# Scores of the grouped heads from split queries and keys, and the convolution's taps moved among the heads

## The chip, the cores and the metric

One core of a Trainium2 chip runs the whole program. The metric is the device time of one execution in microseconds (us). Engines: TensorE (PE, with its weight loads as PEld), VectorE (DVE), ScalarE (ACT), GpSimd (POOL), SyncE (SP). Each takes its own instructions strictly in order; they meet at semaphores.

## The reference

The program is two blocks in a row, for 256 tokens of width 1024. The change is in the second block's layers. There a token stream is projected into four branches; two of them are attention, one is a depthwise convolution:

```
qg, kg, vg = ...                       # 8 query heads, 2 key/value heads, 64 wide ("grouped")
qm, km, vm = ...                       # 8 heads, queries and keys 96 wide ("latent")
o = softmax(q @ concat(k_ctx, k).T * scale) @ concat(v_ctx, v)      # both kinds
conv[t] = b + sum over tap of w[tap] * glu[t + tap - 15]            # 31 taps, 512 channels
x = x + g1 * merge(conv, gate, o_m, o_g);   x = x + g2 * conv_ffn(x)
```

Over two layers three such stages run in full: the context stream of layer 0 (256 keys, no rotary embedding), the main stream of layer 0 and the main stream of layer 1 (both 512 keys, rotary). A fourth, shorter stage has no attention.

## The kernel before

Everything is feature-major: features on the 128 partitions, tokens along the free axis. Weights come by DMA into a ring of three tiles; ACT makes a high part of each half tile (L1839) and DVE the low part (L2583), both in the type fp32r, and TensorE forms high*high + high*low + low*high, three fp32r matmuls in place of one of fp32 (`three`, L825). The trace has two records for each fp32 matmul and one for each fp32r matmul.

`stream(t)` is written three times, once for each engine, and works through one stage; its order is written by hand. `n` counts the full stages, `HEADS` is 16, `MH` is 8: heads j = 0 to 7 are latent, 8 to 15 grouped. `taps(...)` below is `depthwise_conv`. The loop over heads, by engine:

- TensorE: `scores(j)` (L1545) multiplies the queries of two token halves (a stationary of 96 or 64 rows) with the keys (256 or 512 columns), in fp32, into two of six PSUM banks that three heads share in turn; `turn(j)` (L1562) transposes the exponentials; `weigh` (L1579) multiplies with the values, four matmuls of 256 columns at 512 keys and two at 256 keys. Iteration j does turn(j), scores(j+2), weigh for earlier heads. `scores(j+2)` waits until ACT has copied out head j-1. After head 7 and after head 15, `shares` (L1555) transposes the inverse sums: it waits for DVE's `inverse_sums`. scores(10) takes the banks of the first `shares`, and waits until ACT has copied these (`spread_shares`, L2284).
- DVE: `row_max(j+2)` (L3178, L3179), then at set places the splitting of weights (L2583), `inverse_sums` (L3192, L3193), `weighed_heads` (L3199), `low_part` (L3184), and then taps of the depthwise convolution (L3089), one `scalar_tensor_tensor` of 128x256 for each tap and block of 128 channels; each tap of a block adds to the one before.
- ACT: for head j, the copy of the turned head to SBUF (L2303), then the two exponentials of head j+2 (L2291).

Before: `row_max(j+2)` stands ahead of iteration j's taps, `inverse_sums(0)` in iteration 7 ahead of `row_max(9)`, and `inverse_sums(1)` behind the loop. In the rotary stages the taps end with iteration 12: one tap of blocks 0 to 2 in each of iterations 0 to 7, one of block 3 in most of these, four of block 3 in each of iterations 8 to 12. In the stage without rotary only block 3 is left for the loop: two taps in most iterations, three in 10 to 12.

Of the kernel before, what the change touches and what calls it, by code (L numbers as in the profile page):

```python
# [7 lines left out]
F32R = mybir.dt.float32r  # L8
# [6 lines left out]
P = 128  # L15
# [187 lines left out]
def build(nc, d, out, ffn_tiles, stream_tiles):  # L203
# [3 lines left out]
    with ctx:  # L207
# [43 lines left out]
        latent_parts = [parts("latent_high", 25088, 4, S), parts("latent_low", 26112, 4, S)]  # L251
        grouped_parts = [parts("grouped_high", 27264, 4, S), parts("grouped_low", 28288, 4, S)]
        conv_parts = [parts("conv_high", 20992, 4, S), parts("conv_low", 22016, 4, S)]
        branch_parts = [parts("branch_high", 27264, KT, S), parts("branch_low", STREAM_H_AT, KT, S)]
# [331 lines left out]
        def _(pe):  # L586
# [833 lines left out]
            def stream(t):  # L1420
# [117 lines left out]
                def scores(j):  # L1538
                    q, k, _, _ = head(j)
                    if j >= 3:  # L1540
                        pe.wait_ge(s["at_pt"], base + j - 2)
                    if j == MH + 2:
                        pe.wait_ge(s["at_norm"], 5 * n + 2)
                    for tt in range(NT):
                        mm = pe.matmul(ps[:, two_banks(j) + tt, 0:keys], q[:, tt * P:(tt + 1) * P], k, start=True, stop=True)  # L1545
                    mm.then_inc(s["at_s"], 1)
# [19 lines left out]
                def weigh(j, part):  # L1566

                    pe.wait_ge(s["at_pt"], base + j + 2)
                    if j == MH // 2 and 0 in part:
                        pe.wait_ge(s["mm_evac"], mm_n[0])  # L1570
                    if j == MH and 0 in part:

                        pe.wait_ge(s["part_high"], 8 * n + 1)
                    for c in part:
                        for i in (j, j + 1):
                            _, _, b, half = head(i)
                            o = ps[half * HD:(half + 1) * HD, 6 + b // 2, (b % 2) * S:(b % 2 + 1) * S]
                            v = v_m[:, c, i * HD:(i + 1) * HD] if i < MH else v_g[:, c, half * HD:(half + 1) * HD]
                            mm = pe.matmul(o, v, pT[i % 4][:, c, :], start=(c == 0), stop=(c == keys // P - 1), skip_group_check=True)  # L1579
                            if c == keys // P - 1:  # L1580
                                mm.then_inc(s["at_o"], 1)
# [52 lines left out]
                def branch(number, moving, behind=None):  # L1634
                    pe.wait_ge(s["part_low"], 7 * n + number)
                    for p in range(4):
# [25 lines left out]
                upper = [split_block() for _ in range(KT)]  # L1662
                pe.wait_ge(s["part_low"], 7 * n + 5)
                for k in range(4):
# [4 lines left out]
                for q in (2, 3):  # L1669
                    pe.wait_ge(s["part_low"], 7 * n + 4 + q)  # L1670
                    for k in (2 * q, 2 * q + 1):
                        mm = out_product(0, 0, k, upper[k], False)
                    if q == 3:

                        mm.then_inc(s["half_used"], 1)
                    for k in (2 * q, 2 * q + 1):
                        mm = out_product(0, 1, k, lower[k], False)
# [26 lines left out]
        def _(actv):  # L1704
# [466 lines left out]
            def stream(t):  # L2171
# [127 lines left out]
                for j in range(HEADS):  # L2299
# [5 lines left out]
                    if j == MH + 3:  # L2305
                        actv.wait_ge(s["part_high"], 8 * n + 1)
                        a(latent_parts[0][:], weighed, ACT.Copy).then_inc(s["part_high"], 1)
                    if j + 2 < HEADS:
                        exponentials(j + 2)
                    if j == 1:  # L2310
                        keep_last_gates()
                actv.wait_ge(s["part_low"], 7 * n + 1)
                spread_shares(1, two_banks(HEADS))
# [47 lines left out]
        def _(dve):  # L2361
# [693 lines left out]
            def stream(t, mm):  # L3055
# [125 lines left out]
                def low_part(number, into, whole, ms=slice(0, 4)):  # L3181

                    dve.wait_ge(s["part_high"], 8 * n + 1 + number)
                    stt(out=into[1][:, ms, :], in0=whole[:, ms, :], scalar=1.0, in1=into[0][:, ms, :], op0=ALU.mult, op1=ALU.subtract)\  # L3184
# [10 lines left out]
                def weighed_heads(group):  # L3195
# [3 lines left out]
                    tt(weighed, attended, weighed, ALU.mult).then_inc(s[("part_high", "at_norm")[group]], 1)  # L3199

                depthwise_conv((3,), range(4))
                row_max(0)
                lows(t, 45)
                row_max(1)
                for j in range(HEADS):
# [8 lines left out]
                    if j == HEADS - 3:  # L3214
                        low_part(1, latent_parts, weighed)
                    if t["rope"] and j < MH:
                        depthwise_conv((0, 1, 2), range(23 + j, 24 + j))
                        if j != 3:
                            depthwise_conv((3,), range(4 + j - (j > 3), 5 + j - (j > 3)))
                    elif t["rope"] and j < HEADS - 3:  # L3220
                        depthwise_conv((3,), range(11 + 4 * (j - MH), 15 + 4 * (j - MH)))
                    elif not t["rope"] and j != 3 and j < HEADS - 3:
                        depthwise_conv((3,), range(4 + 2 * (j - (j > 3)) + max(0, j - 10), 6 + 2 * (j - (j > 3)) + max(0, j - 9)))
                inverse_sums(1)
# [199 lines left out]
```

## Time and profile before

| | |
|---|---|
| time, 3 runs | median 2585.94 us, 2576.88 to 2588.35 |
| the profiled execution | 2578.61 us, span 2576.8 us, granted clock 1.00 |
| busy: PE, PEld, DVE, ACT, POOL | 2541.6, 2361.9, 2050.4, 1282.6, 58.3 us |
| chain that ended last | PE 86%, DVE 9%, ACT 4%, issue 1%, DMA 0% |
| head loops (first scores to second shares) | about 1270 to 1313, 1728 to 1795, 2246 to 2312 us |

The stages of layer 0 (context), layer 0 (main) and layer 1 (main) are called stage 0, 1 and 3 below. A timeline row gives start, busy time, engine, line and tile, and how many instructions it merges. Instructions of one engine overlap at their ends, so what one costs its engine in a full queue is the distance from its start to the next start. That distance is called its step.

### The profile page before, as it was taken

The numbers are of one execution on the slowest core, as the hardware profiler recorded it, in microseconds if no ns is written. First come the engines' busy times: TensorE is split into PE (matmuls) and PEld (weight loads), VectorE is DVE, ScalarE is ACT, GpSimd is POOL, SyncE is SP. The second block draws the span as 40 slices with busy tenths as digits, with TensorE's granted clock in tenths as the row PEclk, the third lists the DMA queues.
The fourth block names the chain that finished last, engine by engine and source line by source line (L and its number), as shares of the span: only waits on it lengthen the run. The fifth ranks groups of instructions, "written<-read, shape, count | busy, mean of one in ns | idle before, by whom it ended". The sixth has DMA issues, their size and how long they took to land.

```text
span 2576.8 us, 49677 instructions
## 1 busy us (share of the span) xinstructions
PE 2541.6 (99%) x20050; PEld 2361.9 (92%) x20050; DVE 2050.4 (80%) x3059; ACT 1282.6 (50%) x1767; POOL 58.3 (2%) x72
## 2 busy tenths in 40 slices
PE   8999999999999999999999999999999999999999
PEld 8999799999988889998979999885999988859999
DVE  7996589899876369967887876797887877978877
ACT  5445553353353344355565445546544465465543
POOL 0000000000011000000000000000000000000000
PEclk9999999999999999999999999999999999999999
DMA  7764267677532067753424555340355543404554
GB/s 294 287 233 173 90 241 281 236 266 276 217 113 101 18 255 260 262 191 137 164 82 166 193 181 194 131 164 9 140 196 188 187 150 146 164 1 148 196 180 146
DMA packets 61518, 454.60 MB, mean 176 GB/s; under 512 B 6872, under 2 KB 6896, under 8 KB 9280
## 3 DMA queue, kind: packets, MB, share of 16 engines
q1 hardware_dynamic: 54720, 394.24, 42.6%
q0 software_dynamic: 6656, 58.35, 5.8%
q8 instruction: 104, 1.70, 0.3%
q14 instruction: 38, 0.31, 0.0%
HBM read 451.49 MB, written 1.07 MB: 176 GB/s over the span
## 4 chain that ended last, share of the span: by engine, by line
PE 86%; DVE 9%; ACT 4%; issue 1%; DMA 0%; DVEq 0%; SPq 0%; ACTq 0%
PE ps L825 20%; PE ps L658 15%; PE ps L659 15%; PE ps L660 15%; PE ps L1119 3%; PE ps L1545 2%; DVE w_parts L2378 1%; PE ps L1404 1%; DVE half_parts L2583 1%; PE ps L1562 1%; PE ps L600 1%; PE ps L1579 1%; PE ps L1387 1%; PE ps L1472 1%; PE ps L1416 1%
## 5 line engine op out<-in xcount | busy, mean ns | idle before, releaser
L1752 ACT ACTIVATE w_parts<-ring 128x1024 fp32r<-128x1024 f32 x462 | 463.1, 1052 | 370.3 <-PE ps L658 347.8
L658 PE MATMUL ps<-normed_parts,w_parts 128*128 128x256 f32 x2160 | 603.3, 279 | 1.7 <-DVE w_parts L2378 1.7
L659 PE MATMUL ps<-normed_parts,w_parts 128*128 128x256 f32 x2160 | 603.5, 279 | 0.0
L660 PE MATMUL ps<-normed_parts,w_parts 128*128 128x256 f32 x2160 | 602.7, 279 | 0.0
L2378 DVE SCALAR_TENSOR_TENSOR w_parts<-ring,w_parts 128x1024 fp32r<-128x1024 f32 x462 | 544.7, 1220 | 30.8 <-ACT w_parts L1752 30.3
L825 PE MATMUL ps<-stream_high,half_parts 128*128 128x256 f32 x2288 | 437.5, 287 | 3.2 <-DVE half_parts L2583 2.2
L658 PEld LDWEIGHTS ps<-normed_parts,w_parts 128*128 128x128 f32 x2160 | 405.9, 188 | 2.3 <-DVE w_parts L2378 2.3
L660 PEld LDWEIGHTS ps<-normed_parts,w_parts 128*128 128x128 f32 x2160 | 406.0, 188 | 0.0
L659 PEld LDWEIGHTS ps<-normed_parts,w_parts 128*128 128x128 f32 x2160 | 405.9, 188 | 0.0
L825 PEld LDWEIGHTS ps<-stream_high,half_parts 128*128 128x128 f32 x2288 | 358.5, 188 | 9.5 <-issue 7.9
L2583 DVE SCALAR_TENSOR_TENSOR half_parts<-ring,half_parts 128x1024 fp32r<-128x1024 f32 x225 | 272.1, 1214 | 116.1 <-ACT half_parts L1839 115.5
L658 PE MATMUL ps<-act_parts,w_parts 128*128 128x256 f32 x1232 | 344.6, 280 | 0.8 <-DVE w_parts L2378 0.8
L659 PE MATMUL ps<-act_parts,w_parts 128*128 128x256 f32 x1232 | 344.2, 279 | 0.0
L660 PE MATMUL ps<-act_parts,w_parts 128*128 128x256 f32 x1232 | 343.7, 279 | 0.0
L1839 ACT ACTIVATE half_parts<-ring 128x1024 fp32r<-128x1024 f32 x225 | 235.4, 1058 | 187.8 <-PE ps L825 160.7
L825 PE MATMUL ps<-stream_low,half_parts 128*128 128x256 f32 x1144 | 319.5, 279 | 0.0
L2465 DVE CUSTOM_DVE_ANT_0 arena<-arena 128x1024 f32<-128x1024 f32 x192 | 227.2, 1221 | 7.7 <-DVE vec L2545 6.5
L658 PEld LDWEIGHTS ps<-act_parts,w_parts 128*128 128x128 f32 x1232 | 231.5, 188 | 2.0 <-issue 1.5
L660 PEld LDWEIGHTS ps<-act_parts,w_parts 128*128 128x128 f32 x1232 | 231.6, 188 | 0.0
L659 PEld LDWEIGHTS ps<-act_parts,w_parts 128*128 128x128 f32 x1232 | 231.5, 188 | 0.0
L825 PEld LDWEIGHTS ps<-stream_low,half_parts 128*128 128x128 f32 x1144 | 215.4, 188 | 4.3 <-issue 4.1
L3089 DVE SCALAR_TENSOR_TENSOR arena<-arena,vec 128x256 f32<-128x256 f32 x360 | 154.2, 483 | 2.4
(495 smaller groups left out, 3807.1 us busy)
## 6 DMA issues: line engine op xcount, KB each, us to landing
ring<-in_weights SPq DMA_DIRECT2D x373, 1024.0 KB, 4.8
arena<-in_mod_weights POOLq DMA_DIRECT2D x32, 1536.0 KB, 6.9
arena<-in_cond POOLq DMA_DIRECT2D x8, 512.0 KB, 7.5
arena<-toeplitz_rows POOLq DMA_DIRECT2D x1, 1536.0 KB, 10.5
x<-in_x SPq DMA_DIRECT2D x1, 1024.0 KB, 4.9
arena<-in_ctx POOLq DMA_DIRECT2D x1, 1024.0 KB, 5.5
out<-x SPq DMA_DIRECT2D x4, 256.0 KB, 2.6
arena<-in_rope POOLq DMA_DIRECT2D x1, 640.0 KB, 8.7
```

The source lines that it names most:

```text
L658: first = pe.matmul(into, wh, high, start=start, stop=False, skip_group_check=True)
L659: pe.matmul(into, wh, low, start=False, stop=False, skip_group_check=True)
L660: return first, pe.matmul(into, wl, high, start=False, stop=stop, skip_group_check=True)
L825: mm = pe.matmul(into, stationary, moving, start=start and n == 0, stop=stop and n == 2, skip_group_check=True)
L1119: mm = pe.matmul(ps[:, mm_n[0] % 4, m * S:(m + 1) * S], w.take(), mixed[i][:, k, :], start=(k == 0), stop=(k == KT - 1))
L1545: mm = pe.matmul(ps[:, two_banks(j) + tt, 0:keys], q[:, tt * P:(tt + 1) * P], k, start=True, stop=True)
L1752: a(w_parts[:, to, 0, cols], ring[:, at, cols], ACT.Copy).then_inc(s["w_high"], 1)
L1839: a(half_parts[:, u % 3, 0, :], ring[:, tile % RING, half * HALF:(half + 1) * HALF], ACT.Copy).then_inc(s["half_high"], 1)
L2378: return stt(out=out, in0=whole, scalar=1.0, in1=high, op0=ALU.mult, op1=ALU.subtract)
L2465: ins = nc.vector.tensor_tensor_reduce(into, mod_w[half][:, q, :], cond_row[c], 1.0, 0.0, ALU.mult, ALU.add, mod_part[:, at, c:c + 1])
L2583: stt(out=half_parts[:, u % 3, 1, :], in0=ring[:, (t["tile"] + tile) % RING, half * HALF:(half + 1) * HALF], scalar=1.0, in1=half_parts[:, ...
L3089: ins = stt(out=conv[:, b, :], in0=src, scalar=wt, in1=conv[:, b, :], op0=ALU.mult, op1=ALU.add)
```

## The change

The queries and keys of the grouped heads are also split into fp32r parts. For a head whose features lie on one half of the partitions, the stationary holds its high queries on both halves, and the moving operand holds the high keys on the head's own half and the low keys on the other: one matmul over 128 rows gives high*high + high*low. A second one over 64 rows adds low queries * high keys. ACT makes the copies in iterations 0, 2 and 3, DVE the four subtractions (`grouped_lows`) in iteration 4, and scores(8) waits for them. The number of taps is the same; they stand in other iterations, the last of them in iteration 14. Semaphore targets are renumbered for the two signals more.

```diff
@@ buffers
+        grouped_q = [parts("grouped_q_even", STREAM_H_AT + 1024, 4, S),
+                     nc.alloc_sbuf_tensor_at("grouped_q_odd", [P, 4, S], F32R, offset=h_at)]
+        grouped_k = [parts("grouped_k_even", 28160, 2 * S), parts("grouped_k_odd", 28672, 2 * S)]
+        grouped_q_low = parts("grouped_q_low", 27136, 4, S)
+        half_rows = [slice(0, HD), slice(HD, P)]
@@ TensorE, scores(j)
+                    if j == MH:
+                        pe.wait_ge(s["part_low"], 8 * n + 1)
                     for tt in range(NT):
-                        mm = pe.matmul(ps[:, two_banks(j) + tt, 0:keys], q[:, tt * P:(tt + 1) * P], k, start=True, stop=True)
+                        into, tokens = ps[:, two_banks(j) + tt, 0:keys], slice(tt * P, (tt + 1) * P)
+                        if j < MH:
+                            mm = pe.matmul(into, q[:, tokens], k, start=True, stop=True)
+                        else:
+                            pe.matmul(into, grouped_q[half][:, b, tokens], grouped_k[half][:, 0:keys], start=True, stop=False)
+                            mm = pe.matmul(into, grouped_q_low[half_rows[half], b, tokens], grouped_k[half][half_rows[half], 0:keys], start=False, stop=True)
@@ ACT, head loop, after the copy (and before exponentials(j + 2))
+                    if j == 0:
+                        for half, r in enumerate(half_rows):
+                            a(grouped_k[half][r, 0:keys], k_g[r, 0:keys], ACT.Copy)
+                    if j in (2, 3):
+                        for r in half_rows:
+                            ins = a(grouped_q[j - 2][r, :, :], q_g[half_rows[j - 2], :, :], ACT.Copy)
+                        if j == 3:
+                            ins.then_inc(s["part_high"], 1)
@@ DVE
+                def grouped_lows():
+                    dve.wait_ge(s["part_high"], 9 * n + 1)
+                    for half, r in enumerate(half_rows):
+                        stt(out=grouped_k[half][half_rows[1 - half], 0:keys], in0=k_g[r, 0:keys], scalar=1.0, in1=grouped_k[half][r, 0:keys],
+                            op0=ALU.mult, op1=ALU.subtract)
+                        ins = stt(out=grouped_q_low[r, :, :], in0=q_g[r, :, :], scalar=1.0, in1=grouped_q[half][r, :, :], op0=ALU.mult, op1=ALU.subtract)
+                    ins.then_inc(s["part_low"], 1)
+                taps_by = (4, 5, 6, 7, 7, 7, 8, 9, 10, 10, 11, 15, 19, 23, 26, 31) if t["rope"] else (4, 6, 8, 10, 10, 10, 12, 14, 15, 17, 18, 20, 22, 24, 26, 31)
@@ DVE, head loop, after row_max(j + 2)
-                    if t["rope"] and j < MH:
-                        depthwise_conv((0, 1, 2), range(23 + j, 24 + j))
-                        if j != 3:
-                            depthwise_conv((3,), range(4 + j - (j > 3), 5 + j - (j > 3)))
-                    elif t["rope"] and j < HEADS - 3:
-                        depthwise_conv((3,), range(11 + 4 * (j - MH), 15 + 4 * (j - MH)))
-                    elif not t["rope"] and j != 3 and j < HEADS - 3:
-                        depthwise_conv((3,), range(4 + 2 * (j - (j > 3)) + max(0, j - 10), 6 + 2 * (j - (j > 3)) + max(0, j - 9)))
+                    if j == 4:
+                        grouped_lows()
+                    elif t["rope"] and j <= MH:
+                        depthwise_conv((0, 1, 2), range(23 + j - (j > 4), 24 + j - (j > 4)))
+                    if j < HEADS - 1:
+                        depthwise_conv((3,), range(taps_by[j], taps_by[j + 1]))
```

## Rows read from the trace of the kernel before

**Rows 1.** Busy time by engine, from scores(0) to weigh(14) of stage 3.
```profile
2242.00:2315.00 73.00, 72.55 (x417) 43.57 (x415) 55.66 (x99) 49.38 (x92) 0.00 (x0) 1.00 0.09 34
```

**Rows 2.** Timeline of TensorE in stage 3: turn(4), scores(6); scores(10); scores(13) to scores(14); shares(1).
```profile
2267.73 1.09 PE L1562 MATMUL ps<-const,arena 128*128 128x128 f32 x8
2268.66 1.88 PE L1545 MATMUL ps<-arena 96*128 96x512 f32 x4
...
2286.37 1.95 PE L1545 MATMUL ps<-arena 64*128 64x512 f32 x4 [0.25 <-ACT arena L2284]
...
2297.17 1.98 PE L1545 MATMUL ps<-arena 64*128 64x512 f32 x4
2299.08 1.08 PE L1579 MATMUL ps<-arena 128*64 128x256 f32 x8
2300.10 1.09 PE L1562 MATMUL ps<-const,arena 128*128 128x128 f32 x8
2301.12 1.98 PE L1545 MATMUL ps<-arena 64*128 64x512 f32 x4
...
2312.26 1.09 PE L1555 MATMUL ps<-const,arena 128*128 128x128 f32 x8
```

**Rows 3.** Timeline of TensorE in the first block: fp32r matmuls of 512 columns.
```profile
265.36 0.63 PE L825 MATMUL ps<-half_parts,stream_high 128*128 128x512 f32 x2
265.83 0.40 PE L825 MATMUL ps<-half_parts,stream_low 128*128 128x512 f32 x1
```

**Rows 4.** Timeline of ACT in stage 3: copy of head 2, exponentials(4), copy of head 3; high part.
```profile
2263.71 1.03 ACT L2303 ACTIVATE arena<-ps 128x1024 f32<-128x1024 f32 x1
2264.61 0.80 ACT L2291 ACTIVATE arena<-ps,arena 128x512 f32<-128x512 f32 x1
...
2266.12 1.05 ACT L2303 ACTIVATE arena<-ps 128x1024 f32<-128x1024 f32 x1
...
2299.95 1.06 ACT L2307 ACTIVATE latent_high<-arena 128x1024 fp32r<-128x1024 f32 x1
```

**Rows 5.** DVE in stage 3: taps (inverse_sums(0) left out), maximum; weighed heads, taps, maximum, taps.
```profile
2279.62 1.79 DVE L3089 SCALAR_TENSOR_TENSOR arena<-arena,vec 128x256 f32<-128x256 f32 x4
...
2282.23 1.23 DVE L3178 TENSOR_REDUCE arena<-ps 128x2 f32<-128x1024 f32 x1
...
2292.98 1.22 DVE L3199 TENSOR_TENSOR arena<-ps,arena 128x1024 f32<-128x1024 f32 x1
2294.12 2.04 DVE L3089 SCALAR_TENSOR_TENSOR arena<-arena,vec 128x256 f32<-128x256 f32 x4
2296.08 1.22 DVE L3178 TENSOR_REDUCE arena<-ps 128x2 f32<-128x1024 f32 x1
...
2297.41 2.04 DVE L3089 SCALAR_TENSOR_TENSOR arena<-arena,vec 128x256 f32<-128x256 f32 x4
```

**Rows 6.** Timeline of TensorE in stage 0: scores(10) and shares(1).
```profile
1297.20 1.10 PE L1545 MATMUL ps<-arena 64*128 64x256 f32 x4 [0.92 <-ACT arena L2284]
...
1312.95 1.09 PE L1555 MATMUL ps<-const,arena 128*128 128x128 f32 x8
```

**Rows 7.** Timeline of DVE in stage 0: two taps, maximum, three taps.
```profile
1302.00 1.00 DVE L3089 SCALAR_TENSOR_TENSOR arena<-arena,vec 128x256 f32<-128x256 f32 x2
1302.92 0.68 DVE L3178 TENSOR_REDUCE arena<-ps 128x2 f32<-128x512 f32 x1
...
1303.71 1.52 DVE L3089 SCALAR_TENSOR_TENSOR arena<-arena,vec 128x256 f32<-128x256 f32 x3
```

**Rows 8.** Timeline of ACT in stage 0: copy of head 2, exponentials(4), copy of head 3.
```profile
1283.30 0.60 ACT L2303 ACTIVATE arena<-ps 128x512 f32<-128x512 f32 x1
1283.78 0.58 ACT L2291 ACTIVATE arena<-ps,arena 128x256 f32<-128x256 f32 x1
...
1284.86 0.62 ACT L2303 ACTIVATE arena<-ps 128x512 f32<-128x512 f32 x1
```

**Rows 9.** Timeline of DVE in stage 3: the low part of the latent heads.
```profile
2308.43 1.22 DVE L3184 SCALAR_TENSOR_TENSOR latent_low<-arena,latent_high 128x1024 fp32r<-128x1024 f32 x1
```

More of the change, by code:

```diff
@@ L1538, in scores @@
                 def scores(j):
-                    q, k, _, _ = head(j)
+                    q, k, b, half = head(j)
                     if j >= 3:
@@ L1571, in weigh @@
                     if j == MH and 0 in part:
-                        pe.wait_ge(s["part_high"], 8 * n + 1)
+                        pe.wait_ge(s["part_high"], 9 * n + 2)
                     for c in part:
@@ L1634, in branch @@
                 def branch(number, moving, behind=None):
-                    pe.wait_ge(s["part_low"], 7 * n + number)
+                    pe.wait_ge(s["part_low"], 8 * n + 1 + number)
                     for p in range(4):
@@ L1662, in stream @@
                 upper = [split_block() for _ in range(KT)]
-                pe.wait_ge(s["part_low"], 7 * n + 5)
+                pe.wait_ge(s["part_low"], 8 * n + 1 + 5)
                 for k in range(4):
@@ L1669, in stream @@
                 for q in (2, 3):
-                    pe.wait_ge(s["part_low"], 7 * n + 4 + q)
+                    pe.wait_ge(s["part_low"], 8 * n + 1 + 4 + q)
                     for k in (2 * q, 2 * q + 1):
@@ L2305, in stream @@
                     if j == MH + 3:
-                        actv.wait_ge(s["part_high"], 8 * n + 1)
+                        actv.wait_ge(s["part_high"], 9 * n + 2)
                         a(latent_parts[0][:], weighed, ACT.Copy).then_inc(s["part_high"], 1)
+                    if j == 0:
[6 more added lines that the diff above has]
+                            ins.then_inc(s["part_high"], 1)
                     if j + 2 < HEADS:
@@ L2311, in stream @@
                         keep_last_gates()
-                actv.wait_ge(s["part_low"], 7 * n + 1)
+                actv.wait_ge(s["part_low"], 8 * n + 1 + 1)
                 spread_shares(1, two_banks(HEADS))
@@ L3181, in low_part @@
                 def low_part(number, into, whole, ms=slice(0, 4)):
-                    dve.wait_ge(s["part_high"], 8 * n + 1 + number)
+                    dve.wait_ge(s["part_high"], 9 * n + 2 + number)
                     stt(out=into[1][:, ms, :], in0=whole[:, ms, :], scalar=1.0, in1=into[0][:, ms, :], op0=ALU.mult, op1=ALU.subtract)\
```

## The prediction

> **What bounds the kernel now.** I read the chain that ended last first: TensorE holds 86% of it and DMA none, so the question is whether the head loops lie on it too. The busy times of the loop's stretch in stage 3 say yes: TensorE is busy 72.55 of 73 us, DVE 55.66, ACT 49.38 [rows 1]. Here the reader is to see two things. TensorE has no slack, so a cheaper scores step is worth its full price at first; and DVE has only 17 us of slack in the whole stretch, a part of it at the end, where it has nothing to do. Then I read the timelines engine by engine for the steps, and for the two places where engines meet: scores(10), which waited 0.25 us for ACT's copy of the shares [rows 2], and shares(1), which waits for DVE's inverse sums. From shares(1) on the change alters no work, so each stage is judged by when shares(1) starts: 2312.26 in stage 3 [rows 2], 1312.95 in stage 0 [rows 6]. Stage 1 has the form of stage 3 and is counted with its rows.
>
> **TensorE's part.** A 64-row scores step takes 1.91 us at 512 keys, weigh 1.02, turn 1.02 [rows 2]: 3.95 a head. An fp32r matmul of 512 columns takes 0.47 / 2 = 0.235 [rows 3], four of them 0.94. The trace has no head that goes between 128 and 64 rows four times. Its one hint: turn before a 96-row scores took 0.93, before a 64-row one 1.02 [rows 2], so a change of the row count costs about 0.1. The new step lies between 0.94 (changes free) and 1.91 (nothing won). I take 1.2, nearer to the sum of rows, 0.94 plus some 0.3 for the changes. At 256 keys half of the columns gives 0.47 plus the same 0.3, 0.8, against 1.1 before [rows 6]. Taken alone that is 8 x 0.7 = 5.6 us in each rotary stage and 8 x 0.3 = 2.4 in stage 0.
>
> The Trainium skill (TensorEngine Tiling (Array Packing), Key Properties) says that a change of tiling mode drains TensorE. That speaks against this change, which makes four such changes a head. By that rule the step would be above mine; what it would do is the second rival below.
>
> **ACT's part.** Four copies of 64x1024 stand ahead of exponentials(4) and (5). The nearest row is the high part of 128x1024, 1.06 busy [rows 4]; its step is some 0.1 less, 0.95. Half the partitions could make it cheaper only if partitions counted; a lower bound is half, an upper one 1.06. I take 0.95, thus 1.9 in each of iterations 2 and 3. In stage 3 copy(2) starts at 2263.71 and takes 0.90, so exponentials(4) start at 2266.5 and, with the 1.51 of [rows 4], end at 2268.0. turn(4) started at 2267.73 [rows 2] and becomes 2268.05, scores(6) 2269.0 in place of 2268.66. Its step is that of the 96-row form, so row_max(6) starts at 2270.95. The second pair of copies ends at 2268.0 + 0.9 + 1.9 = 2270.8, in time for the subtractions. turn(5) then waits till 2272.4, and TensorE runs some 1 us late up to scores(8). The key copies of iteration 0 lie beside the gate products of TensorE; I take them at 0, and at most 1 us a stage if that cover fails.
>
> **DVE's part.** Steps: row_max 1.33, four taps of one block 1.96 or 0.49 each, weighed heads 1.14 [rows 5]; four mixed taps 1.79 busy, 1.71 as a step with the same 0.08 of overlap that the 2.04 and 1.96 show, and inverse_sums 2282.23 - 2279.62 - 1.71 = 0.90 [rows 5]. The four subtractions have no row of their own. The nearest is the same operation on 128x1024, 1.22 busy [rows 9], a step of 1.14 with the same overlap. Those of 64x1024 lie between a tap's 0.49 and that; I take 1.14. Those of 64x512 lie between the same two, 0.7. Together 3.7 in a rotary stage, 3.3 in stage 0 (keys of 256: 0.49 each). Their low end is 2.0.
>
> *Up to scores(10), stage 3.* row_max(6) ends 2272.3, subtractions 2276.0; then row_max(7), 4 taps, row_max(8), 4 taps, inverse_sums(0), row_max(9) = 3 x 1.33 + 2 x 1.71 + 0.90 = 8.3, all queued without a gap because TensorE's scores(7) to (9) are ready before: 2284.3. Exponentials(9) 1.5 and the copy of the shares (as large as a turned head, 1.0) bring scores(10) to 2286.85, against 2286.37 [rows 2]. So the first two cheap scores gain nothing; shares(0) and scores(10) wait for DVE instead.
>
> *From scores(10) to shares(1), stage 3.* row_max(10) starts at 2286.85 + 1.2 = 2288.05. From there DVE's queue is: six row_max 7.98, three taps in iteration 8 of 0.43 each 1.3, weighed heads 1.14, 21 taps of block 3 (1 + 4 + 4 + 4 + 3 + 5 in iterations 9 to 14) 10.3, low part 1.14 [rows 9], inverse_sums 0.90: 22.75. Behind the taps of iteration 14 stands inverse_sums(1), and for that TensorE waits with shares(1) and weigh(14), ACT with the second copy of the shares. Is DVE ever idle there? In iterations 10 to 12 it needs 1.33 + 1.96 = 3.3 a head, TensorE 1.02 + 1.2 + 1.02 = 3.25: they are level, DVE just behind. So shares(1) starts at 2288.05 + 22.75 = 2310.8: **1.45 us earlier**, in place of 5.6. In the last two iterations TensorE is through early, at about 2309, and stands for the eight taps there.
>
> *Stage 0.* Here the steps are 0.79 for row_max and 0.46 to 0.48 for a tap [rows 7]; copy 0.48, exponentials 1.08 [rows 8]. Copies cost ACT the same 1.9 twice, since the queries are as long. The first pair ends at 1283.30 + 0.48 + 1.9 = 1285.7, exponentials(4) 1286.8, copy(3) and the second pair 1289.2. DVE's subtractions start there and end at 1292.5. row_max(7), 2 taps, row_max(8), 2 taps, inverse_sums(0), row_max(9): 5.1, 1297.6; exponentials(9) and the shares' copy 2.1: scores(10) at 1299.7, against 1297.20 [rows 6]. Then 0.8 to row_max(10) at 1300.5, and the queue: 6 x 0.79, 16 taps of 0.475, weighed heads 1.14, low part 1.14, inverse_sums 0.90 = 15.5, shares(1) at 1316.0: **3.0 us later**.
>
> **The sum.** 2 x (-1.45) + 3.0 = +0.1 us on the profiled execution's 2578.61. That one lies 7.3 us under the median of the three runs, 2585.94, and the shift is carried over to the median: 2586.0. Bounds: if the unknown prices all fall low (scores 0.94, subtractions 2.0, copies half) each rotary stage gains about 1.7 from the subtractions, 0.3 from the scores and 0.5 from ACT more, stage 0 some 3: about -8. If all fall high (scores step 1.9, key copies uncovered) it is about +11: in each rotary stage six scores of 0.7 more, less what the shared queue hides, and 1 us in each stage.
>
> **The rivals.**
>
> *DVE keeps up and TensorE's gain comes through.* For it: DVE's idle 17 us [rows 1], and that the taps left the first grouped heads. Against it: the idle time lies before head 8 and behind the last taps, while the loop now adds 3.7 there. If DVE never ended a wait, each rotary stage would gain 5.6 less the ACT delay 0.5, stage 0 would lose 2.5 - 2.4: 2 x (-5.1) + 0.1 = -10, **2576**.
>
> *Row-count changes drain TensorE.* The place is inside scores(8) to scores(15). A 512-column fp32r matmul is shown 0.40 busy at a step of 0.235 [rows 3], so 0.17 of it is still under way when the next starts; if each of the four changes waited for that, scores would take 0.94 + 0.7 = 1.6. From 1.25 on TensorE, not DVE, is the later one in iterations 10 to 12. Then six scores are 0.4 dearer than forecast, 2.1 to 2.4 us in each rotary stage, row_max(15) comes at about 2305.7, and the taps moved behind it (1.33 + 1.14 + 8 x 0.49 + 0.90 = 7.3) set shares(1) at 2313.0, 0.75 later than before. With 3.5 in stage 0 that is **+5, 2591**. Against it: the 0.09 that the one visible change cost [rows 2]. This is what the page cited above would make of the time.
>
> *The gain is bigger only at the end.* If the eight taps of iterations 13 and 14 fit into the wait for exponentials(15), which end about 3 us before them by my steps, each stage gains 3 more: -9, **2577**. Against it: DVE is in order, and none of its rows has a tap below 0.43.
>
> **Chances.** The forecast, within 4 us of 2586: 0.70. DVE keeps up: 0.07. Taps fit: 0.06. Drain: 0.15. Rest 0.02. The range 2576 to 2592 leaves out the low bound of the first and third with the runs' own spread of 11.5 us, and the far end of the drain. A change of under 0.5% (13 us) can't be told from none; no case alone crosses it, only the spread of runs on top: faster 0.05, same 0.92, slower 0.03.
>
> **What would show it.** Right: 64-row plus 128-row scores at a step near 1.2 in a rotary stage; TensorE idle before shares(0), scores(10) and above all before shares(1), released by DVE's copy of inverse_sums; DVE without idle time from row_max(10) to there; TensorE idle before turn(4) and turn(5) for ACT, near 3 us in all in stage 0. Head loop of stage 0 longer by 3 us, those of stages 1 and 3 shorter by about 1.5. Wrong: rotary stages shorter by over 4 us, scores steps above 1.5, or DVE idle between maxima of the grouped heads.

## The result, and the profile after

The changed kernel takes 2595.09 us (median of 11 runs, 2590.0 to 2602.62), the kernel before 2578.17 on the same chip (11 runs, 2575.73 to 2588.35): ratio 1.0063, interval 1.005 to 1.0075. It is slower, outside the range. The profiled execution took 2597.86 us, with a span of 2596.1 and a mean granted clock of 0.993. A part of the runs of either kernel has a stretch of about 20 us at half clock and is some 8 us longer; mean clocks of 0.9965 or less tell of it, in 7 of 11 runs of the changed kernel and in 17 of 103 runs of the kernel before that were taken beside the experiments.

The first turn, turn(0) (from its weight load), and shares(1) cut the span of the profiled executions into sections. us in each:

| section | before | after |
|---|---|---|
| start to turn(0) of stage 0 | 1276.50 | 1275.10 |
| turn(0) to shares(1), stage 0 | 36.45 | 50.64 |
| on to turn(0) of stage 1 | 423.85 | 425.66 |
| turn(0) to shares(1), stage 1 | 58.07 | 59.58 |
| on to turn(0) of stage 3 | 459.33 | 461.12 |
| turn(0) to shares(1), stage 3 | 58.06 | 59.63 |
| on to the end | 264.54 | 264.37 |

Of 19.3 us more, 14.2 lie in stage 0's loop, 1.5 and 1.6 in the rotary loops, and 1.8 behind each of the first two loops; 1.4 less lie ahead of the first.

Now the windows of the changed kernel (start:end, length, busy us and instructions of PE, PEld, DVE, ACT, POOL, granted clock, DMA share, GB/s). The last one is the loop of stage 3, from scores(0) to shares(1), and answers [rows 1].

```profile
1285.70:1292.50 6.80, 6.73 (x22) 4.26 (x24) 3.81 (x7) 5.88 (x14) 0.00 (x0) 0.51 0.01 2
1292.50:1302.70 10.20, 9.28 (x54) 5.72 (x54) 6.68 (x17) 5.99 (x16) 0.00 (x0) 1.00 0.00 0
1302.70:1323.20 20.50, 20.50 (x67) 11.34 (x66) 12.38 (x26) 11.49 (x31) 0.00 (x0) 0.50 0.00 1
...
1326.60:1330.00 3.40, 3.40 (x16) 1.96 (x14) 1.04 (x1) 1.31 (x2) 0.00 (x0) 0.51 0.00 0
...
1811.30:1814.70 3.40, 3.40 (x18) 2.30 (x17) 0.00 (x0) 1.02 (x1) 0.00 (x0) 0.51 0.00 0
2262.30:2335.00 72.70, 68.02 (x399) 41.93 (x399) 57.45 (x101) 53.78 (x96) 0.00 (x0) 1.00 0.08 30
```

The reader is to see the clock column: four stretches, 34 us in all, at 0.5, the lower of the clock's two levels, 1.2 GHz. The profile of before has none but at its very end, where every profile here has one; those are left out below. In the longest TensorE is busy 20.50 of 20.50 us. In stage 3 TensorE is busy 68.02 us where it was busy 72.55, so the cheaper scores are real; it idles for the difference.

TensorE's timeline in stage 0 (start, busy, engine, line, tile, count, idle time before and its releaser); L1556 and L1557 are the first and second product, L1567 shares, L1574 turn, L1591 weigh. It answers [rows 6].

```profile
1285.77 1.12 PE L1574 MATMUL ps<-const,arena 128*128 128x128 f32 x4 [1.50 <-ACT arena L2303]
...
1293.38 0.36 PE L1556 MATMUL ps<-grouped_k_even,grouped_q_even 128*128 128x256 f32 x1
...
1295.60 0.36 PE L1556 MATMUL ps<-grouped_k_odd,grouped_q_odd 128*128 128x256 f32 x1
...
1300.50 0.36 PE L1556 MATMUL ps<-grouped_k_even,grouped_q_even 128*128 128x256 f32 x1 [0.92 <-ACT arena L2296]
...
1302.76 0.58 PE L1556 MATMUL ps<-grouped_k_odd,grouped_q_odd 128*128 128x256 f32 x1
...
1309.44 0.56 PE L1556 MATMUL ps<-grouped_k_odd,grouped_q_odd 128*128 128x256 f32 x1
...
1313.28 0.56 PE L1556 MATMUL ps<-grouped_k_even,grouped_q_even 128*128 128x256 f32 x1
...
1325.74 1.24 PE L1567 MATMUL ps<-const,arena 128*128 128x128 f32 x8 [1.82 <-DVE arena L3213]
```

A head takes 1295.60 - 1293.38 = 2.22 at full clock and 1313.28 - 1309.44 = 3.84 at half. So by estimate 20.5 x (1 - 2.22 / 3.84) = 8.65 of the 20.5 us are the clock's. DVE, which was to be the bound here, waits for TensorE at half clock, by 2.04 us ahead of each of three maxima (L3198):

```profile
1311.57 0.69 DVE L3198 TENSOR_REDUCE arena<-ps 128x2 f32<-128x512 f32 x1 [2.04 <-PE ps L1557]
```

scores(10) starts 25.40 behind turn(0), where it was 20.70: 4.7 later, the forecast said 2.5. From there to shares(1) it is 25.24 against 15.75, 9.5 more: the clock's 8.65 and 0.85, where the forecast had 0.5.

TensorE in stage 3, one head and shares(1), against [rows 2]:

```profile
2311.77 0.48 PE L1556 MATMUL ps<-grouped_k_even,grouped_q_even 128*128 128x512 f32 x1
2312.18 0.49 PE L1557 MATMUL ps<-grouped_k_even,grouped_q_low 64*128 64x512 f32 x1
2312.60 0.49 PE L1556 MATMUL ps<-grouped_k_even,grouped_q_even 128*128 128x512 f32 x1
2313.02 0.50 PE L1557 MATMUL ps<-grouped_k_even,grouped_q_low 64*128 64x512 f32 x1
2313.45 1.08 PE L1591 MATMUL ps<-arena 128*64 128x256 f32 x8
2314.47 1.09 PE L1574 MATMUL ps<-const,arena 128*128 128x128 f32 x8
2315.32 0.47 PE L1556 MATMUL ps<-grouped_k_odd,grouped_q_odd 128*128 128x512 f32 x1
...
2331.73 1.09 PE L1567 MATMUL ps<-const,arena 128*128 128x128 f32 x8 [2.30 <-DVE arena L3213]
```

The scores step is 2313.45 - 2311.77 = 1.68, in place of the forecast 1.2; each product steps by 0.41 to 0.43, where 0.235 was the price without a change of rows [rows 3]. turn fell from 1.02 to 0.85. A head is 3.55, was 3.95, and was forecast at 3.25.

DVE in stage 3: the first two subtractions (L3225, L3227), row_max(7) behind the fourth, row_max(10), two later maxima (L3198), the last eight taps (L3109), and the end of inverse_sums(1).

```profile
2290.69 0.69 DVE L3225 SCALAR_TENSOR_TENSOR grouped_k_even<-arena,grouped_k_even 64x512 fp32r<-64x512 f32 x1
2291.39 1.22 DVE L3227 SCALAR_TENSOR_TENSOR grouped_q_low<-arena,grouped_q_even 64x1024 fp32r<-64x1024 f32 x1
...
2294.58 1.23 DVE L3198 TENSOR_REDUCE arena<-ps 128x2 f32<-128x1024 f32 x1
...
2307.47 1.23 DVE L3198 TENSOR_REDUCE arena<-ps 128x2 f32<-128x1024 f32 x1 [2.80 <-PE ps L1557]
...
2313.56 1.22 DVE L3198 TENSOR_REDUCE arena<-ps 128x2 f32<-128x1024 f32 x1 [0.60 <-PE ps L1557]
...
2317.10 1.23 DVE L3198 TENSOR_REDUCE arena<-ps 128x2 f32<-128x1024 f32 x1 [0.15 <-PE ps L1557]
...
2326.66 4.12 DVE L3109 SCALAR_TENSOR_TENSOR arena<-arena,vec 128x256 f32<-128x256 f32 x8
...
2330.98 0.69 DVE L3213 COPY arena<-arena 128x1024 f32<-128x1024 f32 x1
```

DVE needs 2294.58 - 2290.69 = 3.9 us for the four subtractions (forecast 3.7). From row_max(10) to shares(1) it is 2331.73 - 2307.47 = 24.26, forecast 22.75: DVE now waits for TensorE in four iterations (1.08 us together, 0.60 the largest), and then holds TensorE for the eight taps. And ACT's copies in stage 0, two pairs:

```profile
1282.38 2.12 ACT L2325 ACTIVATE grouped_q_even<-arena 64x1024 fp32r<-64x1024 f32 x2
...
1286.23 2.12 ACT L2325 ACTIVATE grouped_q_odd<-arena 64x1024 fp32r<-64x1024 f32 x2
```

64x1024 costs as much as the 1.06 of 128x1024 [rows 4]. TensorE waits for ACT by 0.64 us ahead of turn(4) and 0.80 ahead of turn(5) in stage 3, near the forecast; in stage 0 by 1.50 ahead of turn(4) and not at all ahead of turn(5), for at half clock it was late itself.

### The profile page after: what moved, and what is told of

Its sections match the earlier page's. It is cut to its first block, busy times and chain, and to the rows that moved or that the text cites. A ratio compares the mean times of both kernels' runs of the same rounds, so it can differ in the third digit from the quotient of the medians.

```text
span 2596.1 us, 49710 instructions
## 1 busy us (share of the span) xinstructions
PE 2550.3 (98%) x20050; PEld 2370.1 (91%) x20050; DVE 2061.6 (79%) x3071; ACT 1299.4 (50%) x1785; POOL 58.4 (2%) x72
## 4 chain that ended last, share of the span: by engine, by line
PE 85%; DVE 10%; ACT 4%; issue 1%; DMA 0%; DVEq 0%; SPq 0%; ACTq 0%
PE ps L830 19%; PE ps L663 15%; PE ps L664 15%; PE ps L665 15%; PE ps L1124 3%; DVE w_parts L2398 1%; PE ps L1409 1%; DVE half_parts L2603 1%; PE ps L605 1%; PE ps L1574 1%; PE ps L1554 1%; PE ps L1392 1%; DVE arena L3109 1%; PE ps L1591 1%; DVE arena L3198 1%
## 5 line engine op out<-in xcount | busy, mean ns | idle before, releaser
L3109 DVE SCALAR_TENSOR_TENSOR arena<-arena,vec 128x256 f32<-128x256 f32 x360 | 154.2, 482 | 2.4
```

The source lines that it names most:

```text
L3109: ins = stt(out=conv[:, b, :], in0=src, scalar=wt, in1=conv[:, b, :], op0=ALU.mult, op1=ALU.add)
```

## The experiments

All times beside the kernel before on the same chip; "loops" are turn(0) to shares(1) in stages 0, 1 and 3 of the profiled execution, us (before: 36.45, 58.07, 58.06; after: 50.64, 59.58, 59.63). Each kernel ran 4 to 12 times. Behind a time stand its ratio to the kernel before and the interval of that. "..." in a cut of code stands for lines left out.

**e1_full_rows.** Both products over 128 rows; the second then adds low queries * low keys too.

```diff
-mm = pe.matmul(into, grouped_q_low[half_rows[half], b, tokens], grouped_k[half][half_rows[half], 0:keys], ...)
+mm = pe.matmul(into, grouped_q_low[:, b, tokens], grouped_k[half][:, 0:keys], ...)
```

> The second product of a grouped head also takes all 128 rows (low queries of both heads of the pair, high and low keys): two matmuls of the same form, no change of the row count; it adds terms of the size low*low. Theory (a change between 128 and 64 rows costs TensorE a drain): the scores step at 512 keys falls from the 1.69 us of the changed kernel to 0.94 to 1.0, at 256 keys from 1.23 to about 0.5. Rival (the fp32r matmuls on these operands are slow in themselves): it stays at 1.6 to 1.7. DVE's queue sets shares(1) in both, so a rotary stage gains at most 1.5 us; the granted clock in stage 0 falls as before or more. Time 2588 to 2594, against about 2595 of the changed kernel and 2578 of the kernel before.

Measured: 2585.36 us, 1.0019 (1.0006 to 1.0031); loops 42.51, 57.53, 57.61. TensorE in stage 3:

```profile
2309.77 0.48 PE L1556 MATMUL ps<-grouped_k_even,grouped_q_even 128*128 128x512 f32 x1
2310.09 0.39 PE L1557 MATMUL ps<-grouped_k_even,grouped_q_low 128*128 128x512 f32 x1
2310.32 0.40 PE L1556 MATMUL ps<-grouped_k_even,grouped_q_even 128*128 128x512 f32 x1
2310.55 0.40 PE L1557 MATMUL ps<-grouped_k_even,grouped_q_low 128*128 128x512 f32 x1
2310.88 1.08 PE L1591 MATMUL ps<-arena 128*64 128x256 f32 x8
...
2322.51 1.09 PE L1567 MATMUL ps<-const,arena 128*128 128x128 f32 x8 [2.30 <-DVE arena L3213]
```

The same columns, twice the rows in two of four, and the scores step falls from 1.68 to 1.11. The four products step by 0.32, 0.23, 0.23 and 0.33, with changes of the row count by 0.41, 0.42, 0.42 and 0.43: the inner two changes cost 0.19 each, the outer two 0.1, together 0.57. DVE no longer waits, and row_max(10) to shares(1) is 22.79, for a forecast of 22.75. The long half-clock stretch is gone. Left are 6.8 us of half clock around turn(4), 6.8 around shares(1) of stage 0 and 3.4 behind that of stage 1.

**e2_taps_behind.** The taps of the last iteration stand behind inverse_sums(1).

```diff
-                    if j < HEADS - 1:
+                    if j < HEADS - 2:
                         depthwise_conv((3,), range(taps_by[j], taps_by[j + 1]))
                 inverse_sums(1)
+                depthwise_conv((3,), range(taps_by[HEADS - 2], TAPS))
```

> The five taps of iteration 14 stand behind inverse_sums(1). Theory (they hold up shares(1), and TensorE's idle stretch there is what the clock falls on): shares(1) comes 2.3 us earlier after row_max(15), TensorE's wait there (1.8 to 2.3 us) is gone, the half-clock stretches just after shares(1) of stages 0 and 1 are gone; 3 x 2.3 + 2 x 1.7 = 10 us less than the changed kernel, 2585. Rival (the clock falls for the sparse work of the fp32r scores, not for the waits): the half-clock stretches stay, 7 us less.

Measured: 2588.2 us, 1.0039 (1.0026 to 1.0053); loops 48.55, 57.27, 57.25. shares(1) in stage 3 follows weigh with no wait, and the long stretch in stage 0 stays at half clock, while the window behind shares(1) is at full:

```profile
2318.53 1.08 PE L1591 MATMUL ps<-arena 128*64 128x256 f32 x8
2319.55 1.09 PE L1567 MATMUL ps<-const,arena 128*128 128x128 f32 x8
```

```profile
1301.50:1322.00 20.50, 20.50 (x68) 11.22 (x65) 12.08 (x26) 11.49 (x31) 0.00 (x0) 0.50 0.00 0
1323.00:1330.00 7.00, 6.84 (x53) 5.64 (x49) 4.64 (x7) 3.41 (x4) 0.00 (x0) 1.00 0.04 8
```

The taps' wait is worth 2.3 us in each rotary loop, and with it goes the half clock behind shares(1). The long stretch is not the taps' doing.

**e3_fp32_scores.** Copies, subtractions and taps as in the change, the grouped scores one fp32 matmul on 64 rows.

```diff
-                        if j < MH:
+                        if True:
+                            if j >= MH:
+                                q, k = q_m[0:HD, j - MH, :], k_m[0:HD, j - MH, 0:keys]
                             mm = pe.matmul(into, q[:, tokens], k, start=True, stop=True)
```

The operands are those of the latent heads, so the output is another one.

> All copies, subtractions, waits and tap places of the change, but the grouped heads' scores are one fp32 matmul of 64 rows as before (of the latent heads' queries and keys, so the output is another one). Theory A (waits bring the clock down): TensorE still waits 1.5 us before turn(4) in stage 0, and the clock still falls to half there (6.8 us long); stage 0 is 4 to 8 us longer than before. Theory B (the fp32r scores are too light for the clock): no half clock anywhere, stage 0 about 3 us longer. Both: rotary stages 1.5 to 3 us longer than before by the taps behind row_max(15). Time 2586 by B, 2592 by A.

Measured: 2599.26 us, 1.0072 (1.0051 to 1.0092); loops 51.11, 62.12, 62.17, the long stretch at the same place in the profile (2 of 4 runs by mean clock). So it does not need the light fp32r scores; and without the cheaper scores the other parts cost 4 us in each rotary loop.

**e4_rope_only.** The change in the rotary stages alone; stage 0 keeps its fp32 scores and its old taps, with no copies and no subtractions.

```diff
+                        if j < MH or not t["rope"]:
...
+                    if j in (2, 3) and t["rope"]:
...
+                    if j == 4 and t["rope"]:
```

> The change only in the two rotary stages; the stage of the context stream has its old scores and taps. Theory (most of the loss is stage 0 at half clock): stage 0 is back at its old length (42.5 us from scores(0) to shares(1), against 56.7), clock full there; what is left is 1.6 us in each rotary stage and up to 1.7 us of half clock behind shares(1): 2582 to 2584. Rival (the loss is spread): 2588 or more.

Measured: 2582.8 us, 1.0015 (1.0 to 1.0029); loops 36.45, 59.64, 59.62, no half clock in the profile. The loss against before is 3.9 us, of 16.9 for the whole change: three quarters lay in stage 0.

**e5_both_rope.** e4 with e1's and e2's edits.

> Three edits together on the changed kernel: stage 0 keeps the old scores and taps, the second product takes all 128 rows, and the five taps of iteration 14 stand behind inverse_sums(1). Theory (DVE's queue and then TensorE set shares(1)): turn(0) to shares(1) falls from 58.07 us in the kernel before and 57.5 or 57.3 with either edit alone to about 55.2 in each rotary stage; stage 0 at 36.45; no half clock from the waits before shares(1), as there are none. 2 x 2.8 = 5.7 us less than before: 2573, ratio 0.998. Rival (the denser the saving, the more the clock takes back in the rotary stages): half-clock stretches in stages 1 or 3, 2578 or more.

Measured: 2573.59 us, 0.9982 (0.9968 to 0.9996); loops 36.39, 55.20, 55.18. This is 2.9 us under before in each rotary loop.

**e6_pool_copies.** GpSimd makes the copies of the changed kernel, ACT none.

```diff
+                pool.wait_ge(s["roped"], n + 1)
...
+                    nc.gpsimd.tensor_copy(grouped_k[half][r, 0:keys], k_g[r, 0:keys])
+                pool.wait_ge(s["at_t"], HEADS * n + 3)
...
+                        ins = nc.gpsimd.tensor_copy(grouped_q[half][r, :, :], q_g[half_rows[half], :, :])
```

> The changed kernel with the six high copies of the grouped heads on GpSimd in place of ACT. GpSimd took 2.2 us for 128x1024 elsewhere, so the four of 64x1024 end 6 to 9 us after turn(2), about when row_max(6) is over. Theory (TensorE's waits of 1.50 us before turn(4) and on to turn(5), made by ACT's copies, bring the clock down): these waits and the first half-clock stretch of stage 0 (6.8 us long) are gone, turn(0) to shares(1) of stage 0 falls from 50.6 us by 5 at least, rotary stages gain 0.5 to 1. Rival 1 (the clock falls for the light grouped heads): the first stretch goes, the long one of 20.5 us stays and may come earlier. Rival 2: GpSimd's copies are late or slow DVE, and scores(8) waits instead. Time 2584 to 2590.

Measured: 2593.23 us, 1.0058 (1.0042 to 1.0073); loops 47.30, 59.09, 59.14. GpSimd's casts and the window behind:

```profile
1280.71 2.26 POOL L594 CAST grouped_q_even<-arena 64x1024 fp32r<-64x1024 f32 x2 [15.29 <-PE ps L1588]
```

```profile
1301.00:1321.50 20.50, 20.50 (x70) 11.25 (x69) 12.56 (x27) 11.62 (x32) 0.00 (x0) 0.50 0.00 1
```

The waits before turn(4) and turn(5) and the first half-clock stretch are gone; the long one is not, though nothing but the 0.9 us before scores(10), which the kernel before has too [rows 6], and a wait of 1.2 before scores(8) stand ahead of it.

**e7_taps_only.** The kernel before with the taps at their new places.

> The kernel before with only the taps moved to their new iterations. Theory (eight taps now stand between row_max(15) and inverse_sums(1)): TensorE waits for DVE before shares(1), 2.3 us in the rotary stages by row_max 1.34 + low part 1.14 + 8 x 0.49 + 0.90 = 7.3 against TensorE's 5.2 from scores(15) to shares(1); about 2 us in stage 0. All stages 1.5 to 2.5 us longer, clock down at most just behind shares(1): 2583 to 2587. Rival (the tap places cost nothing by themselves, DVE had room): 2578.

Measured: 2589.65 us, 1.0048 (1.0033 to 1.0064); loops 38.97, 60.42, 60.39. shares(1) in stage 3, and the clock around shares(1) in stages 0 and 1:

```profile
2320.09 1.09 PE L1555 MATMUL ps<-const,arena 128*128 128x128 f32 x8 [2.30 <-DVE arena L3193]
```

```profile
1312.00:1318.80 6.80, 5.03 (x21) 3.56 (x22) 2.73 (x5) 1.35 (x2) 0.00 (x0) 0.51 0.00 0
...
1800.10:1803.50 3.40, 3.28 (x16) 2.38 (x18) 0.07 (x1) 1.02 (x1) 0.00 (x0) 0.52 0.00 0
```

The move of the taps alone costs 2.3 us in each rotary loop and 2.5 in stage 0, with the scores of before; the half clock behind the first two loops comes on top.

**e8_all.** The changed kernel with 128 rows, taps behind, copies on GpSimd.

> The changed kernel in all three stages, with 128 rows in the second product, the last five taps behind inverse_sums(1) and the copies on GpSimd. Theory: rotary stages at 54.5 to 55.2 us from turn(0) to shares(1); stage 0, now without ACT's waits, near 35 to 37 if the clock holds and 38 to 41 if it falls once: 2571 to 2577. Rival (stage 0 is too light once its scores are cheap, and the clock falls there whatever the waits): stage 0 above 40, 2578 or more.

Measured: 2572.76 us, 0.9982 (0.9973 to 0.9991); loops 37.06, 54.72, 54.68. TensorE in stage 0, and the windows around:

```profile
1289.92 0.36 PE L1570 MATMUL ps<-grouped_k_even,grouped_q_even 128*128 128x256 f32 x1 [1.22 <-DVE grouped_q_low L3233]
...
1291.98 1.11 PE L1588 MATMUL ps<-const,arena 128*128 128x128 f32 x4 [0.77 <-ACT arena L2317]
```

```profile
1291.60:1295.00 3.40, 3.02 (x13) 2.04 (x14) 3.26 (x10) 2.51 (x8) 0.00 (x0) 0.52 0.00 0
1295.00:1312.00 17.00, 13.93 (x98) 9.04 (x97) 13.20 (x30) 14.08 (x38) 0.00 (x0) 1.00 0.00 1
```

Behind the wait of 1.22 and within that of 0.77 the clock falls, and it is back after 3.4 us, with TensorE less busy (13.93 of 17) than in the stretches of e2 and e6.

**e9_act_copies.** The kernel before with ACT's copies, which nobody reads.

> The kernel before with only ACT's six copies of the grouped heads added, at the change's places; nothing reads them. Scores, taps and DVE's work are those of before. Theory (the copies make TensorE wait before turn(4) and turn(5), 1.5 us in stage 0, and the clock falls there): one half-clock stretch in stage 0 that begins at turn(4) in most runs, 6.8 us long, 3.4 us lost by it, 3 us by the waits themselves in stage 0 and 1 in each rotary stage: 2578 + 8 = 2586. Whether the long stretch at the grouped heads (20.5 us) comes too is open: if it does, the copies alone explain it; if not, it takes the subtractions and taps, or the 64-row fp32r products. Rival (copies are hidden): 2578.

Measured: 2588.34 us, 1.0029 (1.0013 to 1.0044); loops 45.14, 59.71, 59.79. TensorE in stage 0, and the window behind:

```profile
1287.72 0.66 PE L1566 MATMUL ps<-const,arena 128*128 128x128 f32 x4 [1.50 <-ACT arena L2295]
...
1291.57 0.66 PE L1566 MATMUL ps<-const,arena 128*128 128x128 f32 x4 [1.65 <-ACT arena L2295]
```

```profile
1292.80:1306.50 13.70, 13.70 (x47) 7.51 (x46) 6.05 (x14) 7.04 (x19) 0.00 (x0) 0.51 0.00 0
```

In the profiled execution ACT's copies alone cost 1.6 and 1.7 us in the rotary loops and 8.7 in stage 0, the clock's part in it: TensorE waits 1.50 and 1.65 for ACT, and the clock falls 1.2 us behind the second wait, with fp32 scores.

**e10_pool_rope.** e5 with the copies on GpSimd. 

> Rotary stages as in the kernel with all three mends (128 rows in both products, five taps behind inverse_sums(1), copies on GpSimd), stage 0 as in the kernel before. Theory: stage 0 at 36.45 us from turn(0) to shares(1), rotary stages at 54.7, no half clock: 2 x 3.35 = 6.7 less than before, 2571. Rival (stages compensate later, or stage 0's version was worth something): 2573 or more.

Measured: 2572.29 us, 0.9974 (0.9961 to 0.9987); loops 44.45, 54.72, 54.70. The profiled execution had the long stretch, in a stage 0 whose scores are those of the kernel before; by their mean clocks 10 of the 12 runs had not. So that stretch does not need the change.

```profile
1303.80:1324.30 20.50, 20.50 (x66) 10.67 (x66) 12.44 (x25) 10.69 (x30) 0.00 (x0) 0.51 0.00 1
```

**e11_lighter_taps.** e10 with the rotary taps spread otherwise, three an iteration and the last eight behind inverse_sums(1).

```diff
-taps_by = (4, 5, 6, 7, 7, 7, 8, 9, 10, 10, 11, 15, 19, 23, 26, 31)
+taps_by = (4, 5, 6, 7, 7, 7, 8, 9, 10, 10, 11, 14, 17, 20, 23, 31)
```

> As the kernel before it in this call, with three taps instead of four in iterations 10 to 12 and eight behind inverse_sums(1). Theory (DVE's 3.3 us a head in iterations 10 to 12 still bounds, against TensorE's 2.96): each of these heads gains 0.3 and each rotary stage about 1 us, 53.7 us: 2569 to 2570. Rival (the chain scores, maximum, exponentials, turn bounds, or the taps behind hold up weighed_heads(1)): 2571, no gain.

Measured: 2569.45 us, 0.9961 (0.9947 to 0.9976), the best; loops 36.39, 53.65, 53.68. With scores at 1.11 a head takes TensorE 2.96, and DVE 3.3 with four taps: one tap less an iteration gives 1.05 us a loop back.

**e12_pool_full_rows.** e6 with 128 rows.

> The changed kernel with copies on GpSimd and 128 rows in the second product; taps as in the change. It differs from the kernel with GpSimd's copies alone, whose stage 0 ran 20.5 us at half clock, by the row count alone. Theory (the four row changes a head, idle inside for a drain each, are what the clock falls on in the grouped heads): no long half-clock stretch, stage 0 about 40 us in place of 47.3, of it 3 us wait before shares(1); rotary stages 57.0 in place of 59.1: 2582. Rival (the long stretch comes from lighter work or from chance): it stays, 2588.

Measured: 2583.24 us, 1.0013 (0.9998 to 1.0028); loops 39.71, 57.08, 57.08. Against e6 the loops are 11.6 us shorter, as the ratios to before say too, 7.6 of them in stage 0, where two stretches of 3.4 stand for the one of 20.5.

**e13_all_lighter.** e8 with e11's taps.

> The lighter-taps kernel, but with stage 0 in the split form too (128 rows in both products, copies on GpSimd, five taps behind inverse_sums(1)). Theory (128 rows in stage 0's scores keep the long half-clock stretch away): no run with a mean clock below 0.998, where the kernel with stage 0's old scores had 2 of 12 at 0.996; stage 0 at about 37 us, rotary stages 53.7: median 2570, highest below 2577. Rival (the stretch is chance or goes with light work): 2 or 3 runs of 12 at 0.996, or more.

Measured: 2571.1 us, 0.9969 (0.9957 to 0.9981), 2567.62 to 2573.31; loops 37.04, 53.71, 53.66. Equal to e11 within the intervals. Converting stage 0 as well wins nothing (37.04 against 36.39): the wait for the subtractions and the 3.4 us at half clock, both seen in e8, stand against what its cheaper scores give.

**e14_fp32_128_rows.** The kernel before, its grouped fp32 scores over all 128 rows.

```diff
-                    return q_g[r, b, :], k_g[r, 0:keys], b, half
+                    return q_g[:, b, :], k_g[:, 0:keys], b, half
```

> The kernel before, but the grouped heads' fp32 scores take all 128 rows of queries and keys, so they hold the sum of two heads' products and the output is another one; the same number of columns and records. Theory (it is the 64-row scores on which stage 0's clock falls): no run at 0.996, where the kernel before had 16 of 79. The step of scores falls by the 0.1 to 0.2 us of the row changes (1.91 to 1.81, turn before it 1.02 to 0.93), 8 x 0.2 = 1.5 us in each stage: median 2574. Rival (row count is nothing to the clock): 2 or more runs of 12 at 0.996.

Measured: 2576.44 us, 0.9991 (0.9983 to 1.0); loops 36.28, 56.71, 56.67, clock 1.000 in all 12 runs. TensorE in stage 3:

```profile
2295.99 1.09 PE L1562 MATMUL ps<-const,arena 128*128 128x128 f32 x8
2296.92 1.88 PE L1545 MATMUL ps<-arena 128*128 128x512 f32 x4
2298.73 1.08 PE L1579 MATMUL ps<-arena 128*64 128x256 f32 x8
```

turn 0.93 and scores 1.81, against 1.02 and 1.91 on 64 rows [rows 2]: the two changes of a head cost 0.19 together. The rotary loops gain 1.4 us each by it, stage 0 only 0.17. No run of 12 had the long stretch, but beside them the kernel before had it in 2 of 24 only, so this run alone does not tell whether the rows matter to the clock in fp32.

**e15_one_product.** The changed kernel without the second product: no 64-row matmul is left.

> The changed kernel without the second product (the low queries' part is left out of the scores, all copies and subtractions stay). TensorE has the lightest scores of all, two matmuls of 128 rows, and no row change. Theory: like the kernel with 128 rows in both products, the clock falls only behind the waits, means 0.997 to 0.999, no stretch of 20 us; turn(0) to shares(1) of stage 0 about 42, rotary stages 57.5 or less, time 2584. Rival (light work brings the long stretch): means of 0.993 to 0.996 in half of the runs, 2590.

Measured: 2585.39 us, 1.002 (1.0008 to 1.0032); loops 41.58, 57.08, 57.05; half clock in three stretches of 3.4 us, none long. TensorE has the lightest scores of all, and the clock does not fall for long; one run of 10 has a mean of 0.996.

**The long stretch over all kernels**, by runs with a mean clock of 0.9965 or less:

| grouped scores of stage 0 | kernels | runs |
|---|---|---|
| 64 and 128 rows, fp32r | after, e2, e6 | 17 of 23 |
| 64 rows, fp32, behind the copies' waits | e3, e9 | 5 of 14 |
| 64 rows, fp32, as before | before, e4, e5, e10, e11 | 25 of 148 |
| 64 rows, fp32, taps moved | e7 | 0 of 4 |
| 128 rows alone | e1, e8, e12, e13, e14, e15 | 1 of 60 |

The mean clock is a rough count: short stretches lower it too. The kernels of a row differ in more than the rows of the matmuls; the pairs that differ in these alone are after and e1 (7 of 11, 0 of 10) and e6 and e12 (3 of 4, 0 of 10).

## Why the prediction was wrong

It forecast no difference to be measured, 2586.0 (2576 to 2592); the ratio is 1.0063.

**The step that failed** is that of stage 0, "15.5, shares(1) at 1316.0: 3.0 us later". It came out at 14.2. The step let DVE's queue bound the grouped heads, with TensorE at clock 1.00, and no rival let the clock fall. DVE's maxima, taps and sums cost what was listed. But 20.5 us of the grouped heads, and 6.8 around turn(4), ran at half clock, where a head takes TensorE 3.84 us, and DVE waited for it. Of the miss of 11.2 us, 9.0 lie behind scores(10): 8.65 are the clock's, by the estimate above. Of the 2.2 us up to scores(10), 1.2 come with the first stretch (scores(6) took 1.84 in place of 0.96, and row_max(6) ended at 1289.5, 1.2 behind the copies for which the subtractions were to wait), and 0.55 are ACT's dearer copies.

What the runs show of the reason: with 128 rows in every grouped score (e1, e12) the long stretch goes; with copies moved (e6), the last taps behind the sums (e2) or scores made fp32 on 64 rows (e3) it stays. That the waits which ACT's copies add make it more frequent is not shown: e9 has it in 3 of 10 runs, the kernel before beside it in 9 of 35. Nor are the rows told apart from TensorE's waits: in e1 the cheaper scores also leave TensorE waiting by 0.72, 0.48, 0.72 and 0.46 us within stage 0's last grouped heads, where the kernels with the stretch keep it busy.

**TensorE's scores step** was sized at 1.2 and is 1.68. The mechanism was that of my second rival, drain, which had 1.6 by 0.17 a change. By e1, 0.57 of the 1.68 are the changes, for which I had taken some 0.3, and 1.11 are four products without any, for which I had taken 0.94: the first and last of a head step by 0.32, beside fp32 neighbours, and not by 0.235. The hint of 0.09 for one change [rows 2] fits a change between fp32 matmuls (e14: 0.19 for two) and the outer ones here; between two fp32r matmuls a change costs twice that. By the Trainium skill (TensorEngine Tiling (Array Packing), Key Properties) a change of tiling mode drains TensorE; if a change between 64 and 128 rows is one, these runs agree, at 0.1 to 0.19 us each. In stage 0 the scores step rose from 1.06 to 1.23, where 0.8 was forecast, and turn fell from 0.58 to 0.41; so the head stayed at 2.22, and the forecast 2.4 us for cheaper scores came to nothing.

**The rotary loops**: +1.5 and +1.6 in place of -1.45. In stage 3, scores(10) starts 33.59 behind turn(0) (2305.69 - 2272.10), it was 32.17 and 32.65 was forecast: 0.94, most likely for ACT's copies (2.12 a pair, not 1.9) and the mixed scores(8) and (9). Its own step adds 0.58, and the queue from row_max(10) 1.51, for the most part DVE's waits for TensorE (1.08). Together 3.0, the whole miss. That DVE's queue sets shares(1), with eight taps between, was right: 2.30 us of wait, removed by e2, brought back alone by e7.

**Behind the loops** nothing was forecast, because the change alters no work there. But the wait before shares(1) let the clock fall behind it in stages 0 and 1, 3.4 us each; with the wait gone, e2 has neither. Over the whole profiled execution, forecast at +0.1 and measured at +19.3, the miss is 11.2 us in stage 0's loop, 3.0 in each rotary loop and 3.6 behind the loops, less 1.6 ahead of them and at the end. The Trainium skill (TensorE: Matmul & The Clock Gate, HAM oscillation — how this bites in real kernels) says that waits that recur between matmuls bring the clock down, so that the work behind each starts at the low level. The page's waits recur in every tile of a loop and are longer; here single waits stand ahead of the short stretches, of 1.50 us ahead of the first and 1.82 ahead of the third. The rule explains nothing of the long one, in which TensorE waits for nothing.

**Open**: why the long stretch begins where it does and lasts, and why in some runs of one kernel and not in others. In the five profiles that have it (after, e2, e3, e6, e10) it begins 1.5 to 2.9 us behind the start of scores(10), which waits 0.9 us for ACT there. But in eight profiles without it (before among them) scores(10) waits 0.92 us too, so this wait alone does not bring it, and no run takes the wait away alone. The second product on 128 rows is shown to keep it away, by 0 runs in 20 against 10 in 15 in the two pairs above; whether by the rows or by the waits that the cheaper scores leave is not. The carry-over from the profiled execution to the median of the three runs was also off: before ran at 2578.17, near its profiled 2578.61, in the comparison.

## What to carry to other kernels

Price a matmul by what stands beside it: where rows alternate between 64 and 128, each change costs 0.1 to 0.2 us, and 128 rows in all of them can be cheaper than 64 in some. Work put between the last maximum and the sums that TensorE waits for is paid; behind them it was free (e2), and waits of 1.5 to 1.8 us on a busy TensorE were followed by 3.4 to 13.7 us at half clock. An engine that is nearly free (GpSimd here) can make the copies: by that alone little was won (e6), but with 128 rows and the last taps behind the sums e11 takes 0.9961 of the time before.

## What the runs showed that was not expected

- The clock can stay at 1.2 GHz for 20.5 us while TensorE is busy 20.50 of 20.50; e10's profile shows it behind fp32 scores as before.
- A cast or copy to fp32r costs ACT the same for 64x1024 as for 128x1024, 1.06 us; GpSimd takes 1.13 for 64x1024 (two in 2.26).
- turn steps 1.02 ahead of 64-row fp32 scores, 0.93 ahead of 128-row fp32 ones (e14) and 0.85 ahead of 128-row fp32r ones (after), with nothing changed in turn itself.
